# Expert outputs summed in two buffers instead of one, rows of a block in another order, and empty rows passed over by the indirect DMAs

## The reference, cut to what matters

```python
scores = sigmoid(xt @ w_router)
_, idx = top_k(scores + router_bias, 6)          # 6 of 64 experts for each token
gate = scores[idx] / sum * 2.5
out = swiglu(x_pad[tok], w_exp_gu[e], w_exp_down[e]) * g[:, None]   # for each block of 128 rows of one expert
routed = zeros.at[row_tok].add(out)
x = layer_norm(ALPHA * x + routed + shared, ln2_g, ln2_b)
```

## Time and profile before

| | |
|---|---|
| Time, median of 3 runs | 2080.55 us (2080.55 to 2083.68) |
| Time of the profiled execution | 2079.63 us |
| Its span, first to last instruction | 2077.8 us |
| Mean granted TensorE clock | 0.981 |
| TensorE busy | 1959.6 us (94%) |
| VectorE, ScalarE, POOL busy | 929.9, 562.7, 618.8 us |
| Moved by DMA | 365.09 MB, 176 GB/s over the span |

### The profile page before, as it was taken

One profiled execution on the slowest core, in us unless ns is written; L12 is line 12 of the kernel. 1 busy time (PEld: TensorE's weight loads), 2 busy tenths in 40 slices (PEclk: granted clock), 3 DMA queues, 4 the chain that ended last, 5 costly groups with the idle time before them and its releaser, 6 DMA issues.

```text
span 2077.8 us, 23451 instructions
## 1 busy us (share of the span) xinstructions
PE 1959.6 (94%) x7658; PEld 1084.7 (52%) x7658; DVE 929.9 (45%) x2467; ACT 562.7 (27%) x1147; POOL 618.8 (30%) x792
## 2 busy tenths in 40 slices
PE   8998999999999999999999899999999999999990
PEld 6786645666555665556555463444444444444440
DVE  4374465999765533030344743233332332332324
ACT  2223554562566640030233000111111111111114
POOL 0042000101220001101223254545445555555444
PEclk9999999999999999999999999999999999999995
DMA  6031212110110011134211406999999999999995
GB/s 189 3 38 14 64 41 102 41 47 5 26 26 3 1 31 48 44 132 126 103 61 48 155 31 217 376 369 373 381 373 375 378 373 376 375 373 377 375 364 193
DMA packets 130467, 365.09 MB, mean 176 GB/s; under 512 B 34641, under 2 KB 82514, under 8 KB 112594
## 3 DMA queue, kind: packets, MB, share of 16 engines
q1 hardware_dynamic: 105250, 289.80, 37.2%
q0 software_dynamic: 23328, 72.90, 13.6%
q10 hardware_dynamic: 1808, 1.33, 0.2%
HBM read 310.82 MB, written 53.04 MB: 175 GB/s over the span
## 4 chain that ended last, share of the span: by engine, by line
PE 55%; DMA 19%; DVE 8%; issue 7%; POOL 7%; ACT 2%; POOLq 0%; SPq 0%; DVEq 0%; ACTq 0%
DMA arena<-x_d,tid 17%; PE psum L630 11%; PE psum L774 9%; PE psum L792 6%; PE psum L645 4%; POOL arena L1293 3%; PE psum L845 3%; PE psum L444 3%; POOL acc_d L1287 2%; PE psum L479 2%; PE psum L708 2%; ACT arena L1341 2%; DVE arena L2264 2%; DMA acc_d<-arena,sid 2%; PE psum L491 2%
## 5 line engine op out<-in xcount | busy, mean ns | idle before, releaser
L1341 ACT ACTIVATE arena<-psum 128x512 f32<-128x512 f32 (+8 forms) x643 | 286.0, 486 | 1086.6 <-PE psum L918 429.7
L918 PE MATMUL psum<-arena 128*128 128x512 f32 x1088 | 484.3, 598 | 27.8 <-DVE arena L2264 24.9
L918 PEld LDWEIGHTS psum<-arena 128*128 128x128 f32 x1088 | 201.6, 190 | 267.2 <-issue 265.0
L1293 POOL DMA_INDIRECT arena<-x_d,tid x276 | 264.9, 960 | 85.8 <-issue 71.3
L932 PE MATMUL psum<-arena 128*128 128x512 f32 x544 | 244.7, 593 | 0.5 <-ACT arena L1341 0.5
L630 PE MATMUL psum<-arena 128*128 128x384 f32 (+1 forms) x768 | 239.7, 471 | 0.2 <-DMA arena<-in_w_glu 0.2
L2314 DVE TENSOR_TENSOR arena<-arena,psum 128x256 f32<-128x256 f32 x68 | 28.6, 421 | 457.7 <-ACT arena L1341 457.7
L630 PEld LDWEIGHTS psum<-arena 128*128 128x128 f32 x768 | 144.5, 190 | 94.7 <-issue 10.9
L774 PE MATMUL psum<-arena 128*128 128x384 f32 (+1 forms) x576 | 177.7, 472 | 1.1 <-DVE arena L2075 1.1
L2264 DVE STREAM_TRANSPOSE arena<-arena 128x256 f32<-128x256 f32 x272 | 150.3, 610 | 54.7 <-DMA arena<-x_d,tid 53.7
L932 PEld LDWEIGHTS psum<-arena 128*128 128x128 f32 x544 | 103.5, 190 | 130.0 <-issue 129.4
(11 more groups left out here) (313 smaller groups left out, 2148.1 us busy)
## 6 DMA issues: line engine op xcount, KB each, us to landing
arena<-in_w_exp_gu SPq DMA_DIRECT2D x69, 2048.0 KB, 10.4
arena<-in_w_exp_down SPq DMA_DIRECT2D x68, 1024.0 KB, 10.8
arena<-in_w_in SPq DMA_DIRECT2D x24, 512.0 KB, 4.5
arena<-in_x_prompt SPq DMA_DIRECT2D x10, 512.0 KB, 4.2
arena<-x_d,tid POOLq DMA_INDIRECT x276, 8.8
arena<-in_w_glu SPq DMA_DIRECT2D x16, 256.0 KB, 4.9
arena<-in_w_attn_proj SPq DMA_DIRECT2D x16, 256.0 KB, 4.5
arena<-in_w_out SPq DMA_DIRECT2D x1, 4096.0 KB, 14.4
```

The costliest lines, as they stand in the source:

```text
L918: last = mm(psum[:, 2, :], xgT[u][:, k, :], ewg[u][:, k, :], start=k == 0, stop=k == DK - 1)
L1293: pool.indirect_dma_start(xg[u][:, g, :], None, x1_d.rearrange("t (a f) -> (t a) f", a=4), bass.IndirectOffsetOnAxis(ap=tid[u][:, g:g + 1] ...
L1341: return act.activation(dst, src, fn, **kw)
```

## The change

- There are two arrays in HBM, `acc_d[0]` and `acc_d[1]`. Blocks with u = 0 add to the first, those with u = 1 to the second. The first starts from ALPHA * x1 plus the shared expert as before; the second is filled with zeros by two more DMAs on ScalarE's queue, at the place where the zeros behind the rows were written before (4 of these DMAs became 6).
- POOL's wait for the other buffer's scatter is gone, in the loop and behind it. The waits for the same buffer's scatter stay.
- At the end SP loads both arrays (18 DMAs instead of 9), and TensorE adds them, tile by tile, by multiplying each with the identity into three pairs of PSUM banks. VectorE and ScalarE read the sum from PSUM; the weight is read from SBUF and no longer copied.
- Partition p = 16a + 8b + c of a block holds the place (17a + 8b + 16c) mod 128: one `iota` on POOL and two operations of VectorE make that list once, behind `block_and_place`, and the one-hot matrices compare with it instead of with 0 to 127. So the empty places, which are the last of a block, are spread over the partitions.
- Gathers and scatters get a bound. Indices beyond it, those of the empty places, are passed over: nothing is moved for them.
- `gate_shared(2)` runs ahead of `slots(0)` on VectorE and no longer between `slots(4)` and `slots(5)`.

```diff
-        acc_d = dram("acc_d", (ACC, DM))
+        acc_d = [dram(f"acc{u}_d", (ACC, DM)) for u in range(2)]
...
+            for i in range(NT):
+                r = rows(i)
+                pe.wait_ge(s(f"acc_loaded{i}"), 32)
+                if i >= 3:
+                    pe.wait_ge(s("scaled"), i - 2)
+                for j in range(2):
+                    for part_ in (x1, odd_sums):
+                        last = mm(psum[0:r, 2 + 2 * (i % 3) + j, :], ident[0:r, 0:r],
+                                  part_[0:r, i, j * 512:(j + 1) * 512], start=part_ is x1, stop=part_ is odd_sums)
+                last.then_inc(s("total_ready"), 1)
...
             for i in range(NT):
-                ld(x1[0:rows(i), i, :], acc_d[tok(i), :], f"acc_loaded{i}")
+                for u, part_ in enumerate((x1, odd_sums)):
+                    ld(part_[0:rows(i), i, :], acc_d[u][tok(i), :], f"acc_loaded{i}")
...
             for u in range(2):
-                if u == 1:
-                    pool.wait_ge(s("y_stored0"), 16)
-                pool.indirect_dma_start(acc_d, bass.IndirectOffsetOnAxis(ap=sid[u][:, 0:1], axis=0), ln1[:, u, :],
+                pool.indirect_dma_start(acc_d[u], bass.IndirectOffsetOnAxis(ap=sid[u][:, 0:1], axis=0), ln1[:, u, :],
                                         None, compute_op=ALU.add).then_inc(s(f"y_stored{u}"), 16)
+
+            pool.iota(place.rearrange("p (a b c) -> p a b c", a=8, b=2), [[17, 8], [8, 2], [16, 8]], base=0,
+                      channel_multiplier=0, allow_small_or_imprecise_dtypes=True).then_inc(s("constants"), 1)
...
             def scatter(u, rows_):
-                pool.indirect_dma_start(acc_d, bass.IndirectOffsetOnAxis(ap=sid[u][:, 0:1], axis=0), rows_, None,
+
+                pool.indirect_dma_start(acc_d[u], bass.IndirectOffsetOnAxis(ap=sid[u][:, 0:1], axis=0), rows_, None,
+                                        bounds_check=T - 1, oob_is_err=False,
                                         compute_op=ALU.add).then_inc(s(f"y_stored{u}"), 16)
...
                     pool.indirect_dma_start(xg[u][:, g, :], None, x1_d.rearrange("t (a f) -> (t a) f", a=4),
-                                            bass.IndirectOffsetOnAxis(ap=tid[u][:, g:g + 1], axis=0)
-                                            ).then_inc(s(f"xg_loaded{u}"), 16)
+                                            bass.IndirectOffsetOnAxis(ap=tid[u][:, g:g + 1], axis=0),
+                                            bounds_check=4 * T - 1, oob_is_err=False).then_inc(s(f"xg_loaded{u}"), 16)
...
-                    pool.wait_ge(s(f"y_stored{1 - u}"), ip * 16 + 16 + 16 * u)
                     carry_wait()
                     scatter(u, yb[u])
...
-                pool.wait_ge(s(f"y_stored{1 - u}"), last_pair * 16 + 16 + 16 * u)
...
-                        act.dma_start(acc_d[T:ACC, half], zeros).then_inc(s("acc_cleared"), 16)
+                        act.dma_start(acc_d[1][:, half].rearrange("(b p) f -> p b f", p=DEC),
+                                      zeros[0:DEC].unsqueeze(1).broadcast_to([DEC, ACC // DEC, 512])
+                                      ).then_inc(s("acc_cleared"), 16)
+                        act.dma_start(acc_d[0][T:ACC, half], zeros).then_inc(s("acc_cleared"), 16)
...
-            for j in range(2):
-                f(psum[:, j, :], ln2[:, 0, j * 512:(j + 1) * 512]).then_inc(s("weight_placed"), 1)
...
+                dve.wait_ge(s("constants"), 11)
+                step(ts(wrapped, place, P - 0.5, -float(P), ALU.is_ge, ALU.mult))
+                step(tt(place, place, wrapped, ALU.add))
...
             dve.wait_ge(s("x1_stored"), 16 * NT)
+            gate_shared(2)
             for i in range(NT + 1):
-                if 2 <= i + 1 < NT and i > 0:
+                if 3 <= i + 1 < NT:
                     gate_shared(i + 1)
...
-                    ts(o[:, 0:P], iota64[0:r, :], sin_[0:r, m // MK, k:k + 1], None, ALU.is_equal)
+                    ts(o[:, 0:P], place[0:r, :], sin_[0:r, m // MK, k:k + 1], None, ALU.is_equal)
...
             def final_moments(i):
-                r, x = rows(i), x1[0:rows(i), i, :]
-                dve.wait_ge(s(f"acc_loaded{i}"), 16)
+                r, x = rows(i), total(i)
+                dve.wait_ge(s("total_ready"), i + 1)
...
-                    stt(x, x, fin[0:r, i, 0:1], weight[0:r, :], ALU.subtract, ALU.mult).then_inc(s("scaled"), 1)
+                    stt(y, x, fin[0:r, i, 0:1], weight[0:r, :], ALU.subtract, ALU.mult).then_inc(s("scaled"), 1)
```

More of the change, by code:

```diff
@@ L231, in layer_program @@
         empty = at(49152, NBP)
+        place, wrapped = at(47616, P), at(47616 + P, P)
         ln2 = at(10752, 2, DM)
         fin = at(47104, NT, 6)
-        weight = psum[:, 0:2, :].rearrange("p b n -> p (b n)")
+        odd_sums = at(15424, NT, DM)
+        total = lambda i: psum[0:rows(i), 2 + 2 * (i % 3):4 + 2 * (i % 3), :].rearrange("p b n -> p (b n)")
         eps = at(47160, 1)
@@ L1125, in _ @@
                 sp.wait_ge(s("base_ready"), i + 1)
-                ld(acc_d[tok(i), :], x1[0:rows(i), i, :], "base_stored")
+                ld(acc_d[0][tok(i), :], x1[0:rows(i), i, :], "base_stored")
             for q, name in enumerate(("ln2_g", "ln2_b")):
@@ L1261, in _ @@
                 tt(x, x, ln1[0:r, 1, :], ALU.add).then_inc(s("x1_ready"), 1)
-            pool.wait_ge(s("acc_cleared"), 16 * 4)
+            pool.wait_ge(s("acc_cleared"), 16 * 6)
             pool.wait_ge(s("dump_ready"), 2)
             for u in range(2):
-                if u == 1:
-                    pool.wait_ge(s("y_stored0"), 16)
-                pool.indirect_dma_start(acc_d, bass.IndirectOffsetOnAxis(ap=sid[u][:, 0:1], axis=0), ln1[:, u, :],
+                pool.indirect_dma_start(acc_d[u], bass.IndirectOffsetOnAxis(ap=sid[u][:, 0:1], axis=0), ln1[:, u, :],
                                         None, compute_op=ALU.add).then_inc(s(f"y_stored{u}"), 16)
+            pool.iota(place.rearrange("p (a b c) -> p a b c", a=8, b=2), [[17, 8], [8, 2], [16, 8]], base=0,
+                      channel_multiplier=0, allow_small_or_imprecise_dtypes=True).then_inc(s("constants"), 1)
             pool.wait_ge(s("slots_ready"), 1)
@@ L1522, in take_qk_turned @@
                     act.wait_ge(s("h_stored"), 64)
-                    act.wait_ge(s("acc_cleared"), 16 * 4)
+                    act.wait_ge(s("acc_cleared"), 16 * 6)
                 k0 = i * P if i < NT - 1 else SEQ + PAST
@@ L1640, in _ @@
             half_y(1, last_pair * 2 + 2)
-            act.wait_ge(s("ln2_loaded"), 32)
-            for j in range(2):
-                f(psum[:, j, :], ln2[:, 0, j * 512:(j + 1) * 512]).then_inc(s("weight_placed"), 1)
             moments = [0]
@@ L1656, in final_std @@
                 if i in MOMENTS_BY_SCALAR:
-                    x, unread = x1[0:r, i, :], psum[0:r, 2:4, :].rearrange("p b n -> p (b n)")
-                    act.wait_ge(s(f"acc_loaded{i}"), 16)
+                    x, unread = total(i), psum[0:r, 0:2, :].rearrange("p b n -> p (b n)")
+                    act.wait_ge(s("total_ready"), i + 1)
                     moment(f(unread, x, ACT.Copy, accum_out=m(4)))
@@ L2351, in scale_by_weight @@
             def scale_by_weight(i):
-                r, x = rows(i), x1[0:rows(i), i, :]
+                r, x, y, weight = rows(i), total(i), x1[0:rows(i), i, :], ln2[:, 0, :]
                 if i == 0:
-                    dve.wait_ge(s("weight_placed"), 2)
+                    dve.wait_ge(s("ln2_loaded"), 32)
                 if i in MOMENTS_BY_SCALAR:
                     dve.wait_ge(s("std_ready"), NT + i + 1)
-                    stt(x, x, fin[0:r, i, 5:6], weight[0:r, :], ALU.add, ALU.mult).then_inc(s("scaled"), 1)
+                    stt(y, x, fin[0:r, i, 5:6], weight[0:r, :], ALU.add, ALU.mult).then_inc(s("scaled"), 1)
                 else:
                     dve.wait_ge(s("var_ready"), NT + by_vector_no(i))
-                    stt(x, x, fin[0:r, i, 0:1], weight[0:r, :], ALU.subtract, ALU.mult).then_inc(s("scaled"), 1)
+                    stt(y, x, fin[0:r, i, 0:1], weight[0:r, :], ALU.subtract, ALU.mult).then_inc(s("scaled"), 1)
                     dve.wait_ge(s("std_ready"), NT + i + 1)
```

## The result

The changed kernel takes 2101.7 us (median of 4 runs, 2099.2 to 2102.0) against 2081.2 before (4 runs, 2080.6 to 2083.7): a ratio of 1.0094, with a 95% interval of 1.0078 to 1.011. It is 0.9% slower where 1.2% faster was forecast. The profiled execution has a span of 2100.0 us against 2077.8, 22.2 more.

A forecast was written before the change was run, and what follows sets the result against it. It took the loop as bound by full DMA engines at 11.13 us a block, with the scatter chain and TensorE close. 2079.6 - 32.2 - 1.5 + 10.4 = 2056.3, with 0.9 for the median 2057.2 us; range 2048 to 2085.

The forecast's parts named there:

- What bounds the kernel now: Block loop: scatter chain 11.1 us, DMA engines 11.13, TensorE 10.52 a block; a shorter chain alone gives nothing.
- Empty places passed over: Block loop: a quarter fewer rows in POOL's queue shortens the step from 11.13 to 10.65 us, 32.2 us less.
- Order of partitions: List of places: costs some 0.4 us, hidden; makes the 25% come off all 16 DMA engines alike.
- the fullest DMA engine stays full: Rival, block loop: the 25% don't come off all 16 engines alike, so little or nothing is gained; 10%.
- Zeros for the second array: Ahead of the loop, near 304 us: 5.0 MB more while DMA engines are idle from 310 to 320 us; cost 0.
- The end: After the last block: TensorE's sums of both arrays set the pace; 10.4 us more, 2.9 gained by the wait included.
- gate_shared(2) earlier: Ahead of the loop: TensorE's 9.49 us wait goes, but POOL's token matrices come late next; 1.5 us saved.
- Price of an indirect DMA with a bound: POOL's gathers and scatters in the loop: even a dearer price, at most 2.7 us more, hides; taken as 0.

The follow-up runs named there:

- Run 2: Changed kernel with nothing passed over and the old order of partitions, zero fills issued by SP; two arrays, no wait for the other scatter: 2093.1 us, ratio 1.0051.
- run 11: Changed kernel with only the order of places replaced by one made for groups of four partitions: 2073.6 us, ratio 0.996.
- run 5: Kernel before (one array, wait kept) with bounds on gathers and scatters and an order made for groups of four partitions: 2048.1 us, ratio 0.9835.
- run 8: Kernel before with gathers and scatters over partitions 0 to 95 only, no bounds, leaving out a quarter of each block's rows: 2079.9 us, ratio 0.999.
- run 4: Kernel before (one array, wait kept) with bounds on gathers and scatters and the change's order of partitions: 2071.5 us, ratio 0.9952.
- Run 1: Changed kernel with the second array's zero fills issued by SP behind its weight loads, not by ScalarE: 2090.2 us, ratio 1.0039.
- run 3: Kernel before (one array, wait kept) with only the bounds on gathers and scatters added, old order of partitions: 2083.6 us, ratio 1.0004.
- run 12: Kernel before with gate_shared(2) moved early and nothing else: 2081.7 us, ratio 0.9999.
- run 10: Changed kernel with zero fills issued by SP and the order made for groups of four partitions: 2059.0 us, ratio 0.9888.

## Why the prediction was wrong

*What bounds the kernel now: right.* It said that the scatters' chain and the DMA engines lie at the same 11.13 us, and that taking the wait away alone gives nothing. Run 2 has 11.13.

*Empty places passed over: this step failed.* The prediction took 0.75 x 3.97 us for POOL's queue on every engine and a step of 10.65, 32.2 us less. The loop gave 1.0. POOL's share did fall, though to 0.85 and not 0.75 of its time, and the weights' queue took back 0.37 of the 0.60 us a block that this freed. What failed is the assumption in *Order of partitions* that this order lets the 25% shorten the step: only another order does (run 11 on the changed kernel, 10.73; run 5, 10.67, where 10.65 was reckoned). The rival "the fullest DMA engine stays full" had 10% for a loop that gives little or nothing back, and the loop gave 1.0 us. Its reason, that the 25% don't come off all 16 engines alike, fits the orders tried (11.08 and 10.67 with one array, 11.11 and 10.73 with two); it stays argued: no record names an engine, and run 8, whose gather packets can be shared out evenly, six rows to each of 16, has a step of 11.06. The prediction also held the weights' time fixed while POOL's queue shrank, but it rose from 7.45 to 7.82 us a block after the change, and to 8.26 in run 8. The chance was what went wrong: that two of three groupings are even was a guess about which partitions share an engine, which no row of before and no run shows. Runs 4 and 5 speak against the two by which the change's order is even, by runs of 8 and by every 16th. That the list is made row by row, as the rival says, the packets bear out (one packet a row for a scatter, one piece a row in a gather's packet), but it decides nothing here.

*Zeros for the second array: this step failed.* It was priced at 0, "the engines are idle from 310 to 320 us". The loop starts 13.7 us later although the gate below gives 0.7 back, so the zeros cost some 14.4. TensorE's trace has 13.6 of it, 10.33 of standing and 3.3 at half clock (4.26 and 3.87 us for matmuls of 1.99 and 2.85). The DMA engines were idle, but the queue that issues wasn't: the question was what stands behind the DMAs on ScalarE, and that is the emptying of PSUM, which stood for 15.85 us. Run 1 takes 11.5 us back.

*The end: right in its pace, with some luck in the sum.* 10.4 us were reckoned, 9.5 measured; 30.9 us of matmuls and 1.6 for the clock against 33.2 us; the first pair of tiles 4.9 us after the first load, as measured (2047.16 to 2052.04). But the first load goes 19.3 us after the last block's start, where 22.2 were reckoned, because the last scatter lands 2.75 us after its issue, where it took 5.95 before; 1.2 us more behind the last sum and 0.7 more in the sums take two thirds of that back. Against runs that pass places over with one array the price is higher, 72 against 57 to 58 us, because the last scatter then lands in 2.72 us as well (runs 3, 4 and 5) and the wait ahead of it costs little. The 2.9 us that the second array was to save in the end are not to be had beside the bounds.

*gate_shared(2) earlier: mechanism right, size a little off.* 1.5 us were reckoned, 0.7 shown. The one-hot matrices decided it, as the working has it, though not POOL's alone: in run 12 TensorE's waits at L891 are for those of VectorE, 0.92 us apart, and in the changed kernel for those of both.

*Price of an indirect DMA with a bound: right.* It was taken as 0. Gathers and scatters of the changed kernel, in the page's groups:

```profile
L1313 POOL DMA_INDIRECT arena<-x_d,tid x276 | 280.8, 1017 | 86.4 <-issue 80.1
...
L1306 POOL DMA_INDIRECT acc_d<-arena,sid x68 | 110.9, 1631 | 38.7 <-POOL carry L1319 19.4
```

A gather takes 1017 ns against 960, a scatter the same; POOL had the room.

The sum for the profiled execution with both failed steps in their place: 2056.3 + (32.2 - 1.0) + (14.4 + 0.8) - 0.9 = 2101.8, where 14.4 is the zeros, 0.8 what the gate gave less than reckoned and 0.9 the end. The profiled execution took 2101.8, as it must, since the terms are read from it. The test is run 10: with both causes removed it is 2059.0, where 2057.2 was forecast. With one removed (run 11) it is 2073.6.

## What to carry to other kernels

Rows that are left out of a DMA need not save time: here the same bytes left out gave 11.21, 11.08 or 10.67 us a block by the partitions that they were left out of. Try more than one order before spreading the gaps for good, since the share averaged over the engines didn't tell them apart (1.01 in run 4, 1.02 in run 5). And don't count on the other queue's time staying as it was: it took back more than half of what POOL's queue saved, after the change (0.37 of 0.60 us a block) and in run 8 (0.81 of 0.91). A DMA costs the engine that issues it, too (16.8 us of ScalarE's queue here, with the DMA engines idle before); put such large ones where nothing urgent stands behind them on that queue. And before a wait is removed from a loop whose DMA engines are full, or a stalled step is moved forward, price what is late next: here both removals were worth nothing by themselves.

## What was unexpected of the hardware

- Traffic that is left out doesn't show as idle DMA engines. With a quarter of POOL's bytes gone the share is still 1.01 after the change and 1.02 in run 8, and the weights' queue takes 70.4% of the time for 166.34 MB and 74.7% for 168.54, in place of 66.9% for 167.07. The packets of 16 KB are longer in the records, 644 and 689 ns in the mean against 616; what lengthens them no run shows.
- A gather over 96 partitions has as many packets as one over 128, 32 (run 8: 16 of 4 KB and 16 of 2 KB; before, 32 of 4 KB), and with a quarter fewer bytes in POOL's queue the step was 11.06 us in place of 11.13.
- Issuing two zero fills of 2.4 MB and four small DMAs held ScalarE's queue for 16.8 us; four small ones alone took 2.7 us before. On SP, single issues behind the zeros took 7.95 and 9.52 us.
- The last scatter of run 5, its empty places passed over, landed 2.72 us after its issue; before it took 5.95 us.
